# Tokens gathered and scattered by plain fp32 products in a two-block forward pass, and a ring of thirteen expert slabs

## What is computed

```python
def grouped_moe(x, router_w, router_bias, w_gate_up, w_down):
    t = x.reshape(-1, D)
    scores = jax.nn.sigmoid((t @ router_w).astype(jnp.float32))
    # the best group of 4 experts, then the best two in it (by biased scores)
    ...
    weights = sel / jnp.sum(sel, -1, keepdims=True)
    gates = jnp.sum(jax.nn.one_hot(top_idx, N_EXPERTS) * weights[..., None], 1)
    h = jnp.einsum('td,edf->tef', t, w_gate_up)
    a = jax.nn.silu(h[..., :D_EXPERT]) * h[..., D_EXPERT:] * gates[..., None]
    return jnp.einsum('tef,efd->td', a, w_down)
```

## Time and profile before

| | |
|---|---|
| median of 3 runs | 1567.66 us (1567.39 to 1568.59) |
| the profiled execution | 1570.28 us, its span 1568.5 us |
| TensorE busy | 1537.0 us (98%) |
| DVE, ACT, POOL busy | 834.4, 706.1, 88.6 us |
| moved by DMA | 328.31 MB, mean 209 GB/s |
| granted TensorE clock, mean | 0.997 |

### The profile page before, as it was taken

How to read it: one execution, slowest core, us unless ns; L and a number is a source line. 1 busy time by engine, 2 the same in 40 slices (tenths; PEclk the granted TensorE clock), 3 DMA queues, 4 the chain that set the end, 5 groups by cost and what they waited for, 6 DMA issues and landing times.

```text
span 1568.5 us, 20466 instructions
## 1 busy us (share of the span) xinstructions
PE 1537.0 (98%) x7540; PEld 1175.6 (75%) x7540; DVE 834.4 (53%) x1114; ACT 706.1 (45%) x1147; POOL 88.6 (6%) x158
## 2 busy tenths in 40 slices
PE   8999999999999999999999999999999999999998
PEld 7876444877544588888888888888888888888886
DVE  4665215476422745556567555555555656755554
ACT  5662112683212434445374544454444546554443
POOL 2320000050000000000100000000000020000000
PEclk9999999999999999999999999999999999999999
DMA  7536997545699555556535656546555652655551
GB/s 243 201 119 261 409 412 279 168 167 211 277 416 413 200 190 183 187 193 203 161 109 187 197 187 193 186 146 212 189 187 179 208 185 87 221 188 184 187 190 57
DMA packets 165986, 328.31 MB, mean 209 GB/s; under 512 B 8874, under 2 KB 106896, under 8 KB 152992
## 3 DMA queue, kind: packets, MB, share of 16 engines
q1 hardware_dynamic: 164992, 323.52, 59.5%
q0 software_dynamic: 928, 3.89, 0.8%
HBM read 326.33 MB, written 1.05 MB: 209 GB/s over the span
## 4 chain that ended last, share of the span: by engine, by line
PE 92%; DVE 2%; ACT 2%; DMA 1%; issue 1%; DVEq 0%; POOL 0%; SPq 0%; POOLq 0%; ACTq 0%
PE bank L439 23%; PE bank L441 23%; PE bank L440 23%; PE bank L1198 7%; PE bank L1246 3%; PE bank L833 1%; PE bank L1158 1%; PE bank L1159 1%; PE bank L1254 1%; PE bank L862 1%; PE bank L1255 1%; DMA sb_xT<-exp_w_down 1%; PE bank L910 1%; DMA sb_raw<-w_in 1%; DVE sb_wlo L435 1%
## 5 line engine op out<-in xcount | busy, mean ns | idle before, releaser
L435 DVE TENSOR_TENSOR sb_wlo<-sb_raw,sb_whi 128x1024 fp32r<-128x1024 f32 (+2 forms) x419 | 483.3, 1197 | 345.3 <-ACT sb_whi L428 341.2
L428 ACT ACTIVATE sb_whi<-sb_raw 128x1024 fp32r<-128x1024 f32 (+2 forms) x419 | 407.9, 1027 | 318.5 <-PE bank L441 307.3
L439 PE MATMUL bank<-sb_whi,sb_op_hi 128*128 128x512 f32 (+2 forms) x1216 | 476.9, 392 | 6.4 <-DVE sb_op_lo L1982 3.5
L441 PE MATMUL bank<-sb_whi,sb_op_lo 128*128 128x512 f32 (+2 forms) x1216 | 469.2, 386 | 0.0
L440 PE MATMUL bank<-sb_wlo,sb_op_hi 128*128 128x512 f32 (+2 forms) x1216 | 468.5, 385 | 0.0
L439 PEld LDWEIGHTS bank<-sb_whi,sb_op_hi 128*128 128x128 f32 x1216 | 229.7, 189 | 53.5 <-issue 4.3
L441 PEld LDWEIGHTS bank<-sb_whi,sb_op_lo 128*128 128x128 f32 x1216 | 229.4, 189 | 46.4
L440 PEld LDWEIGHTS bank<-sb_wlo,sb_op_hi 128*128 128x128 f32 x1216 | 229.9, 189 | 43.0
L439 PE MATMUL bank<-sb_whi,sb_lat_hi 128*128 128x512 f32 (+2 forms) x456 | 175.7, 385 | 1.0 <-DVE sb_wlo L435 1.0
L441 PE MATMUL bank<-sb_whi,sb_lat_lo 128*128 128x512 f32 (+2 forms) x456 | 174.5, 383 | 0.0
L440 PE MATMUL bank<-sb_wlo,sb_lat_hi 128*128 128x512 f32 (+2 forms) x456 | 174.4, 382 | 0.0
(11 more groups left out here) (260 smaller groups left out, 1332.5 us busy)
## 6 DMA issues: line engine op xcount, KB each, us to landing
sb_raw<-ffn_w SPq DMA_DIRECT2D x264, 512.0 KB, 4.3
sb_moe<-exp_w_gate_up SPq DMA_DIRECT2D x50, 1024.0 KB, 8.6
sb_raw<-w_in SPq DMA_DIRECT2D x84, 512.0 KB, 4.7
sb_moe<-exp_w_down SPq DMA_DIRECT2D x26, 1024.0 KB, 8.6
sb_raw<-w_out SPq DMA_DIRECT2D x32, 512.0 KB, 4.2
sb_per_block<-exp_w_gate_up SPq DMA_DIRECT2D x8, 1024.0 KB, 7.8
sb_xT<-exp_w_gate_up SPq DMA_DIRECT2D x6, 1024.0 KB, 9.3
sb_xT<-exp_w_down SPq DMA_DIRECT2D x4, 1024.0 KB, 11.1
```

What stands on the lines that cost most here:

```text
L428: nc.scalar.activation(h, r, ACT.Copy).then_inc(hi_made.sem, 1)
L435: nc.vector.tensor_tensor(o, r, h.bitcast(F32), ALU.subtract).then_inc(lo_made.sem, 1)
L439: nc.tensor.matmul(ps, hi, wh, start=first, stop=False)
L441: return nc.tensor.matmul(ps, lo, wh, start=False, stop=last)
```

## The change

- `x` is no longer split for the gather: `xs_hi`, `xs_lo`, `token_hi` and `token_lo` are gone. `gather` takes block k straight from `x`, every fourth column (`of_slab`), in one plain fp32 product with `in_slot`, which is fp32 now.
- The gates go into the selection matrix: after the gather of a half is done DVE multiplies `in_slot` by the gates in place (`gated(0)` before pair 0, `gated(1)` in pair 3), and the transposes of `pair_slots` carry them into `of_slot`. The gate products (L1215), their copies on ACT and the gate in `of_pair` are gone.
- y isn't split: ACT copies the first 512 columns, DVE the second, into one of four buffers `y_out`; `scatter` is one plain fp32 product. `of_slot` lies in its own buffer `places`. Both take the memory of the operand buffers.
- The memory of `xs_hi` and `xs_lo` becomes two more slots: `MOE_RING` = 13, and the slots have new numbers, so that other buffers come first and last.

```diff
-MOE_RING = 3 * RING + 2
-RAW_SLOT, WHI_SLOT, WLO_SLOT, BLOCK_SLOT, XT_SLOT = (4, 5, 10), (6, 8, 0), (7, 9, 1), 2, 3
+MOE_RING = 3 * RING + 4
+RAW_SLOT, WHI_SLOT, WLO_SLOT = (9, 10, 5), (11, 1, 7), (12, 2, 8)
+BLOCK_SLOT, XT_SLOT, FREE_SLOT = 0, 6, (3, 4)
...
+                for slot in FREE_SLOT:
+                    number = slab_number(0, S1, l, S1_OUT)
+                    expert_slab(slot, lambda: sp.wait_ge(slab_done.sem, number + (1 + RING)))
...
-                    nc.tensor.matmul(b[:, :], xs_hi[:, ch, k, :], to, start=ch == 0, stop=False)
-                    return nc.tensor.matmul(b[:, :], xs_lo[:, ch, k, :], to, start=False, stop=ch == 1)
+                    return nc.tensor.matmul(b[:, :], of_slab(x[:, ch, :], k), to, start=ch == 0, stop=ch == 1)
...
-                    if p == 0:
-                        wait(F, "gates", l, 1)
-                        wait(F, "in_slot", l, 4)
-                    elif p == 1:
-                        wait(F, "of_slot", l, 1)
-                    elif p <= 3:
+                    if p % 4 == 0:
+                        wait(F, "in_gated", l, p // 2 + 2)
+                    if p in (2, 3):
                         wait(F, "xg_d", l, 5 + 2 * p)
+                    elif p:
+                        wait(F, "of_slot", l, p)
                     for ch in range(NC):
-                        nc.tensor.transpose(bank[5][:, ch * P:ch * P + P], to[ch], ident)
-                    for ch in range(NC):
-                        i = nc.tensor.matmul(bank[5][:, T:T + 2], to[ch], gates[:, ch, 2 * p:2 * p + 2], start=ch == 0, stop=ch == 1)
+                        i = nc.tensor.transpose(bank[5][:, ch * P:ch * P + P], to[ch], ident)
...
                 def scatter(p, ch, nh):
-                    wait(F, "y_lo", l, 2 * p + nh + 1)
-                    hi, lo = (y[:, 512 * nh:512 * nh + 512] for y in pair_y[p])
-                    to = of_slot[p][:, ch * P:ch * P + P]
-                    nc.tensor.matmul(ybank(ch, nh)[:, :], to, hi, start=False, stop=False)
-                    i = nc.tensor.matmul(ybank(ch, nh)[:, :], to, lo, start=False, stop=p == PAIRS - 1)
+                    wait(F, "of_slot", l, p + 1)
+                    wait(F, ("y_a", "y_d")[nh], l, p + 1)
+                    i = nc.tensor.matmul(ybank(ch, nh)[:, :], of_slot[p][:, ch * P:ch * P + P], pair_y[p][:, 512 * nh:512 * nh + 512],
+                                         start=False, stop=p == PAIRS - 1)
...
-                def down_hi(p, nh):
-                    if nh == 0:
-                        wait(F, "y0_a", l, p + 1)
-                        wait(F, "y0_b", l, p + 1)
-                    else:
-                        moe_done(act, l, down_slab(p))
-                        moe_done(act, l, down_slab(p) + 1)
-                    nc.scalar.activation(pair_y[p][0][:, 512 * nh:512 * nh + 512], bank[6 + nh][:, :], ACT.Copy).then_inc(F["y_hi"].sem, 1)
+                def down_out(p):
+                    wait(F, "y0_a", l, p + 1)
+                    wait(F, "y0_b", l, p + 1)
+                    nc.scalar.activation(pair_y[p][:, 0:512], bank[6][:, :], ACT.Copy).then_inc(F["y_a"].sem, 1)
...
                 slots(0, 0)
-                token_lo(1, 0)
                 slots(0, 1)
-                token_lo(1, 1)
...
+                def gated(half):
+
+                    dve.drain()
+                    for ch in range(NC):
+                        v = in_slot[:, ch, 8 * half:8 * half + 8, :]
+                        tt(v, v, gates[:, ch, 8 * half:8 * half + 8].unsqueeze(2).to_broadcast([P, 8, CAP]), ALU.mult).then_inc(F["in_gated"].sem, 1)
+
+                gated(0)
...
-                def down_lo(p, nh):
-                    wait(F, "y_hi", l, 2 * p + nh + 1)
-                    hi, lo = (y[:, 512 * nh:512 * nh + 512] for y in pair_y[p])
-                    tt(lo, bank[6 + nh][:, :], hi.bitcast(F32), ALU.subtract).then_inc(F["y_lo"].sem, 1)
+                def down_out(p):
+                    moe_done(dve, l, down_slab(p))
+                    moe_done(dve, l, down_slab(p) + 1)
+                    nc.vector.tensor_copy(pair_y[p][:, 512:1024], bank[7][:, :]).then_inc(F["y_d"].sem, 1)
...
                         if p:
-                            down_lo(p - 1, 1)
+                            down_out(p - 1)
+                        if p == 3:
+                            gated(1)
```

More of the change, by code:

```diff
@@ L210, in program @@
         x = sb("x", [P, NC, D])
[L211 to L214, removed]
+        with ExitStack() as operands:
+            op_hi, op_lo, lat_hi, lat_lo = (operands.enter_context(nc.sbuf_tensor("sb_" + name, [P, n, T], F32R))
+                                            for name, n in (("op_hi", DK), ("op_lo", DK), ("lat_hi", 5), ("lat_lo", 5)))
+        y_out, places = sb("y_out", [P, 4, D]), sb("places", [P, 10, T])
         act_hi, act_lo = lat_hi[:, 0:2, :], lat_lo[:, 0:2, :]
@@ L241, in program @@
         xT = sb("xT", [P, DK, T])
[L242 to L247, removed]
+        free = [sb(f"moe{3 * RING + i}", [P, SLAB]) for i in range(2)]
+        in_slot = sb("in_slot", [P, NC, NE, CAP])
+        pair_y = [y_out[:, p % 4, :] for p in range(PAIRS)]
         xg = sb("xg", [P, 2, DK, 8 * CAP])
-        of_slot = [lat_hi[:, p, :] if p < 5 else lat_lo[:, p - 5, :] for p in range(PAIRS)]
+        of_slot = [places[:, p, :] for p in range(PAIRS)]
         xg_flat = xg[:, :, :, :].rearrange("p h k n -> p (h k n)")
         moe = [None] * MOE_RING
-        for slots, own in ((RAW_SLOT, slabs[0:3]), (WHI_SLOT, slabs[3:6]), (WLO_SLOT, slabs[6:9])):
+        for slots, own in ((RAW_SLOT, slabs[0:3]), (WHI_SLOT, slabs[3:6]), (WLO_SLOT, slabs[6:9]), (FREE_SLOT, free)):
             for i, t in zip(slots, own):
@@ L387, in program @@
             ("xT_a", 3, 0), ("xT_d", 1, 0), ("logit", 8, 0), ("logit_out", 2, 0), ("folded", 2, 0), ("routed", 1, 0),
[L388 to L389 removed]
+            ("hot", 1, 0), ("counted", 1, 0), ("ranked", 1, 0), ("sized", 1, 0), ("in_slot", 4, 0), ("in_gated", 4, 0),
+            ("gathered", 2 * DK, 0), ("xg_a", 4, 0), ("xg_d", 12, 0), ("slot", PAIRS, 0), ("of_slot", PAIRS, 0),
             ("sg", PAIRS, 0), ("a", PAIRS, 0), ("aT", PAIRS, 0), ("aT_out", PAIRS, 0),
             ("done_a", MOE // 2, MOE // 2), ("done_b", MOE // 2, MOE // 2), ("y0_a", PAIRS, 0), ("y0_b", PAIRS, 0),
[L392 removed]
+            ("y_a", PAIRS, 0), ("y_d", PAIRS, 0), ("y", 4, 0), ("turned", 4, 0), ("xT2", 4, 0),
         ):
@@ L1165, in early_gather @@
                         gather(0, k, gather_bank(k), 0)
-                    wait(F, "xs_lo", l, 3)
                     wait(F, "in_slot", l, 2)
@@ L1241, in pair_down @@
                         if p:
-                            wait(F, "y_lo", l, 2 * p - 1 + nh)
+                            wait(F, ("y_a", "y_d")[nh], l, p)
                         for f in range(2):
@@ L1719, in _ @@
                 logit_out(0)
-                token_hi(0)
                 routing_out(2)
@@ L2303, in _ @@
                     following(1, (1,))
-                    for nh in range(2):
-                        down_lo(PAIRS - 1, nh)
+                    down_out(PAIRS - 1)
                 def next_lo(h):
```

48 lines of the change are left out of this document (14 added, 34 removed).

## The result

The changed kernel takes 1614.03 us, the median of four runs, against 1568.12 us for the kernel before on the same chip: 1.0294 times as long, interval [1.0281, 1.0307]. The forecast was 1611.5, with a range of 1605 to 1621. The profiled execution has a span of 1613.3 us, 44.8 more than before; +43.8 was forecast.

A forecast was written before the change was run, and what follows sets the result against it. TensorE was taken to bound both expert stages, transfers close behind. Per layer 12.8 + 12.8 - 2.7 - 0.2, 0.3 off, is 22.4; two layers less 1.0 give +43.8 on 1567.66: 1611.5 us, range 1605 to 1621.

The forecast's parts named there:

- The two prices: TensorE products over 512 columns: a hi and lo fp32r pair takes 0.457 us, a plain fp32 product 0.857, +0.40 a call.
- The gather: Token gather of each expert stage: 32 calls a layer become plain fp32 products, all on the path, +12.8 us a layer.
- The scatter: Scatter of the eight pairs' outputs: 32 calls a layer become plain, shown in full, norm stays covered, +12.8 us a layer.
- The gate products: Small products in each pair's chain go: 0.34 us a pair, eight pairs, -2.7 us a layer.
- Splitting x: ACT copies and DVE subtractions go; only DVE's earlier routing start reaches the path, -0.2 us a layer.
- DVE's new work: Two gating multiplications and a drain before pair 0's slot transposes, 4.1 us of cover for 1.5 us: zero cost.
- Thirteen slots: Two more slabs ahead of pair 0 gain nothing; new slot numbers remove the second layer's last-slab wait, -1.0 us once.
- The clock: Low granted clock after the second layer, losing at most 3.3 us, kept unchanged; 3 us either way in the spread.
- (a): Gather's strided weight loads are exposed: up to 18 us more, 1620 to 1630 us; chance 0.09.
- (b): Transfers pace the expert stages, added products fill slab waits, two slabs save 5.0 us a layer: 1557.7 us; chance 0.02.
- (c): Plain products in gather and scatter go as one instruction at fp32r pace: -17.4 us a layer, 1532 us; chance 0.01.
- (d): Some additions replace TensorE pauses, up to 4 us a layer: 1603.5 us; chance 0.05.

The follow-up runs named there:

- hi_only_11: The kernel before with only the hi product of each pair in gather and scatter, the lo products left out; 1564.86 us, ratio 0.9976.
- x_packed: The changed kernel with the gather's weights read as packed blocks of 128 columns of x instead of every fourth column; 1612.39 us.
- ring11: The changed kernel with the eleven slots and slot numbers of before; 1613.21 us.
- plain_gather: The kernel before with only the gather turned into one plain fp32 product with strided weights from x; 1594.46 us, ratio 1.0168.
- light_11: The changed kernel with its scatter as one fp32r product, the lo part left out, and the eleven slots of before; 1589.76 us.
- gates_cheap: The kernel before with one fp32r gate product on four columns, reordered subtractions from x, and a raw reload put behind the last slab; 1570.79 us.
- gates_no_swap: The kernel before with one fp32r gate product on four columns and reordered subtractions from x, SyncE's queue unedited; 1566.10 us, ratio 0.9987.
- no_gate_products: The kernel before without the gate products, ACT copying a one instead of the gate; 1563.88 us, ratio 0.9975.

## Why the prediction was right, point by point

- **What bounds the kernel.** Right for this change, since what TensorE was given showed in full. The sentence "the transfers close behind" was truer than its use: hi_only_11 shows that a forecast in the other direction, by the same sum, would have been off by some 12 us a layer, 7.7 of them (first layer) ahead of the last down, which waits for its slab. A sign of it was in the rows from the start, in the one wait for a slab and the share of 1.01.
- **The two prices.** 0.857 us for a plain product and 0.457 for a pair held: pair 4 took 14.78 us and a last pair 13.06, forecast 14.8 and 13.1.
- **The gather**, +12.8: measured +13.35. This term was mis-sized, by 0.55 us a layer. "Up 0 starts 13.8 us after the first" was 14.04 by the timeline. x_packed accounts for more of it than is missing: 0.85 us a layer is what a strided load costs at each block's start. The step that was off was to take the strided load at exactly 0 because it fits under a product; the first of a block has no product to hide under.
- **The scatter**, +12.8: measured +12.47. Also what stands behind: the norm was covered, the transposes follow the scatter without a wait.
- **The gate products**, -2.7: the changed kernel's pairs are shorter by just these 0.34 us. In the kernel before, their removal alone brought 2.0 and 0.5.
- **Splitting x**, -0.2: didn't come at in_slot, as the fillers end when they did. A start of the gather 0.13 us sooner behind its in_slot write (0.25 instead of 0.39 us) is all that shows.
- **DVE's new work** cost nothing. The gated writes end at 162.2 us, and the slot transposes are due at 164.63. The cover was as read: 3.8 us from DVE's last in_slot write (160.79), where 4.1 was forecast.
- **Thirteen slots**: no gain from the slots, as said. The second layer's 1.0 us went, as said, but the reason given was one of two. The new slot numbers do let the slab go earlier; ring11 and plain_gather show that without them it lands in time too, since in these longer stages it takes less time from issue to landing.
- **The sum of a layer**: 22.4 forecast, 22.87 measured; the second, less 1.0, 21.4 and 21.89. The two together are 0.96 us over the forecast: the gather's 0.55 a layer over, the scatter 0.33 under; the 0.3 that the sum took off for the pace of the fp32r step did not show apart from these.
- **The clock** was kept as it was, and in sum was: +1.4 us between the stages and -1.3 behind them in the profiled execution. Which executions have a dip, and how deep, I can't derive; in the runs here it is worth up to 3 us.
- **The rivals.** (a) exists at a tenth of its size. (b), with 1557.7 us, is wrong for this change; that the transfers set the pace is right about the kernel before as soon as work is removed. (c) and (d) are excluded by the steps and the waits: 0.43 us a step, and the only wait in reach is the same 0.6 us. The forecast DMA share of 0.95 was 0.84 to 0.92.

**What stays open:** what sets the low-clock stretches outside the stages; and which part of the median's +45.9 us, beyond the stages' +44.8, belongs to them.

## What to carry to other kernels

Where a busy engine and a busy ring of transfers run side by side, the sum of engine time is a good forecast in one direction only: what is added shows, what is removed can meet the next limit within a microsecond or two, as it did here from the kernel before (1.8 and 2.9 of 14.7 us); from the changed kernel, 22.9 us above it, 17.2 of 20.1 us came off. Look at the waits and the share to see how near it is, and price additions and removals apart. A load or a copy that fits under its neighbour is free in the middle of a run of products, and not at its start: count the starts.

## What the runs showed of the hardware

- A weight load of 128x128 fp32 with 16 bytes between its elements took 309 to 311 ns (median of all, mean in the first stage), packed 188 to 190. This is less than the doubling that ACT's copy showed. The Trainium skill, "SBUF — State Buffer", section "Door 1: The DMA port swizzle", says that accesses which go to a new 16-byte line each pay for it. Weight loads do pay, 1.64 times, and the kernel pays it only where nothing runs beside them.
- One 1 MB slab needs 2.5 us of the DMA engines at 420 GB/s, but the last slab of a stage took 13.85 us from issue to landing, 15.74 in light_11 and 15.91 in hi_only_11, with the reload ahead of it in SyncE's queue. In ring11, with the same reload ahead and the issue at the same point behind down 5, it took 10.1. So the point of issue is one part of it, and the length of the landing another.
- A wait of 2 to 4 us ahead of down 7 can cost up to 3 us more behind it, in a lower granted clock. Down 7 took 6.62 and 6.11 us behind waits of 3.9 and 4.3 (hi_only_11), 5.94 behind 4.0 (light_11, first stage), 5.20 behind 2.6 (gates_cheap, first) and 5.35 behind 2.0 (gates_no_swap, second). But it took 3.65 behind 3.6 (light_11, second), 3.1 (no_gate_products, second), 2.6 (gates_cheap, second) and 1.0. What tells the cases apart stays open.
